# A two-layer decoder step on one core: the chunks of a loop body take their 264 columns in four orders

## What is computed

```python
def _layer(x, ...):
    xn = _rms_norm(x, g_pre_mix)
    proj = xn @ w_in                       # 2048 x IN_WIDTH
    ...                                    # retention, mLSTM, pooling on the parts of proj
    mixed = jnp.concatenate([ret_out, mlstm_out, pool_out], axis=-1).astype(x.dtype) @ w_out
    x = x + _rms_norm(mixed, g_post_mix)
    hn = _rms_norm(x, g_pre_ffn)
    ff = (jax.nn.silu(hn @ w_ffn_gate) * (hn @ w_ffn_up)) @ w_ffn_down
    x = x + _rms_norm(ff, g_post_ffn)
```

## Time and profile before

| | |
|---|---|
| two timed runs | 2467.01 and 2466.32 us, median 2466.66 us |
| the profiled execution, first to last instruction (its span) | 2466.6 us |
| TensorE, share of the span with a matmul in flight | 99% |
| TensorE, share of the span with a weight load in flight | 97% |
| VectorE, ScalarE, GpSimd, share of the span busy | 57%, 44%, 10% |
| mean granted TensorE clock over the span | 0.995 of full |
| bytes moved by DMA | 443.87 MB, mean 180 GB/s |

### The profile page before, as it was taken

The page is one execution under the profiler, slowest core; times in us unless marked ns, Lnnn a source line. Parts: engine busy times, 40 slices in busy tenths (PEclk is TensorE's granted clock), DMA queues, the critical chain, the costliest instruction groups (busy, mean ns, idle before and its releaser), DMA issues.

```text
span 2466.6 us, 49136 instructions
## 1 busy us (share of the span) xinstructions
PE 2435.6 (99%) x20166; PEld 2387.1 (97%) x20166; DVE 1417.3 (57%) x1721; ACT 1088.0 (44%) x1419; POOL 246.2 (10%) x202
## 2 busy tenths in 40 slices
PE   9999999999999999999999999999999999999997
PEld 8999999899999999999999999998999999999997
DVE  5787564755544455554567866646555445555444
ACT  5444654543333343444444456545344333343443
POOL 1001334000000000002100014340000000000021
PEclk9999999999999999999999999999999999999999
DMA  8455545355545655545645555454555455555453
GB/s 301 164 172 197 196 164 187 137 180 177 187 159 185 202 174 184 183 159 184 222 151 169 173 200 197 167 175 139 185 182 177 167 183 195 187 175 182 163 185 130
DMA packets 71902, 443.87 MB, mean 180 GB/s; under 512 B 8656, under 2 KB 8880, under 8 KB 33136
## 3 DMA queue, kind: packets, MB, share of 16 engines
q1 hardware_dynamic: 64656, 415.40, 49.6%
q0 software_dynamic: 6992, 26.82, 3.5%
q10 hardware_dynamic: 144, 0.08, 0.0%
HBM read 427.10 MB, written 15.16 MB: 179 GB/s over the span
## 4 chain that ended last, share of the span: by engine, by line
PE 95%; DVE 3%; ACT 1%; issue 0%; DMA 0%; DVEq 0%; ACTq 0%
PE bank L572 86%; PE bank L550 1%; PE bank L551 1%; PE bank L552 1%; PE bank L651 1%; DVE work L1326 1%; PE bank L539 0%; DVE x L1333 0%; DVE wlo L1306 0%; PE bank L603 0%; PE bank L604 0%; PE bank L622 0%; PE bank L514 0%; DVE rstd L1319 0%; PE bank L816 0%
## 5 line engine op out<-in xcount | busy, mean ns | idle before, releaser
L1306 DVE TENSOR_TENSOR wlo<-raw,whi 128x2048 fp32r<-128x2048 f32 (+1 forms) x402 | 836.8, 2082 | 512.7 <-ACT whi L941 512.5
L941 ACT ACTIVATE whi<-raw 128x2048 fp32r<-128x2048 f32 (+1 forms) x406 | 709.4, 1747 | 883.8 <-PE bank L572 833.2
L572 PE MATMUL bank<-ahi,wlo 128*128 128x264 f32 x4096 | 537.9, 284 | 0.0
L572 PE MATMUL bank<-ahi,whi 128*128 128x264 f32 x4032 | 533.3, 285 | 0.0
L572 PE MATMUL bank<-alo,whi 128*128 128x264 f32 x4032 | 528.3, 284 | 0.0
L572 PEld LDWEIGHTS bank<-ahi,wlo 128*128 128x128 f32 x4096 | 512.2, 188 | 0.0
L572 PEld LDWEIGHTS bank<-ahi,whi 128*128 128x128 f32 x4032 | 505.0, 188 | 7.1 <-issue 3.1
L572 PEld LDWEIGHTS bank<-alo,whi 128*128 128x128 f32 x4032 | 503.9, 188 | 0.0
L572 PE MATMUL bank<-hhi,wlo 128*128 128x264 f32 x1392 | 190.1, 284 | 0.0
L572 PE MATMUL bank<-hlo,whi 128*128 128x264 f32 x1392 | 188.7, 283 | 0.0
L572 PE MATMUL bank<-hhi,whi 128*128 128x264 f32 x1392 | 188.6, 283 | 0.0
(11 more groups left out here) (311 smaller groups left out, 1817.2 us busy)
## 6 DMA issues: line engine op xcount, KB each, us to landing
raw<-w_gu SPq DMA_DIRECT2D x176, 1024.0 KB, 4.8
raw<-w_in SPq DMA_DIRECT2D x89, 1024.0 KB, 5.0
raw<-w_dn SPq DMA_DIRECT2D x128, 704.0 KB, 4.0
raw<-w_out SPq DMA_DIRECT2D x32, 1024.0 KB, 4.9
work<-s_ret POOLq DMA_DIRECT2D x12, 512.0 KB, 3.7
ret_s<-work POOLq DMA_DIRECT2D x12, 512.0 KB, 3.0
proj<-s_c POOLq DMA_DIRECT2D x8, 576.0 KB, 5.5
c_s<-proj POOLq DMA_DIRECT2D x8, 576.0 KB, 4.1
```

The costliest lines, as they stand in the source:

```text
L572: mm = pe.matmul(out, weights[:, w], operand(tile)[of], start=start and part == 0 and k == 0, stop=stop and not late and part == 2 and k = ...
L941: act.activation(high[:, 0:words], raw[:, slot, 0:words], ACT.Copy).then_inc(*hi_made.up)
L1306: dve.tensor_tensor(wlo[:, slot, w], raw[:, slot, w], high[:, w].bitcast(F32), ALU.subtract)\
```

## The change

`chunk` gets a parameter `view`. A new helper `columns(view, ap)` rearranges the 264 columns of an access pattern: it cuts them into a parts of b blocks of c columns and goes through block 0 of each part, then block 1 of each part, and so on. View 0 leaves the pattern as it is; view 1 has 3 parts of 11 blocks of 8 columns, view 2 has 2 parts of 33 blocks of 4, view 3 has 2 parts of 66 blocks of 2. The helper is applied to the result's pattern in PSUM and to the streamed operand's in SBUF alike. `whole` passes view = j; all other callers keep view 0.

```diff
+                def columns(view, ap):
+                    if view:
+                        return ap.rearrange("p (a b c) -> p b a c", a=(1, 3, 2, 2)[view], c=(264, 8, 4, 2)[view])
+                    return ap
+
+                def chunk(n, slot, hi_slot, out, operand, ks, start, stop, last_ready=None, norm=None, middle=None, view=0):
+
+                    out = columns(view, out)
...
-                            mm = pe.matmul(out, weights[:, w], operand(tile)[of], start=start and part == 0 and k == 0,
+                            mm = pe.matmul(out, weights[:, w], columns(view, operand(tile)[of]), start=start and part == 0 and k == 0,
                                            stop=stop and not late and part == 2 and k == len(ks) - 1)
...
-                def whole_tile(c, o, slot, j, operand, hi_slot=0, norm=None, middle=None):
+                def whole_tile(c, o, slot, j, operand, hi_slot=0, norm=None, middle=None, view=0):
...
                     chunk(c, slot, hi_slot, bank[j][:, 0:TOK], operand, range(KT), True, True, norm=norm,
-                          middle=middle)
+                          middle=middle, view=view)
...
                             whole_tile(l * N_CHUNKS + c0 + i * RAW + j, l * N_TILES + o0 + i * RAW + j, (at_rest + j) % RAW, j, operand,
-                                       hi_slot=j % HI)
+                                       hi_slot=j % HI, view=j)
```

More of the change, by code:

```diff
@@ L555, in high_of @@
                     return whi_spare if hi_slot is None else whi[:, hi_slot]
-                def chunk(n, slot, hi_slot, out, operand, ks, start, stop, last_ready=None, norm=None, middle=None):
+                def columns(view, ap):
[4 more added lines that the diff above has]
+                    out = columns(view, out)
                     high, low = high_of(hi_slot), wlo[:, slot]
```

## The result

The changed kernel takes 2604.02 us (2602.32 to 2605.71, 2 runs) against 2466.66: 137 us more, ratio 1.0553 with a 95% interval of 1.0536 to 1.0570. The forecast was 2467 within 2425 to 2700, with 0.34 on slower. So the time is inside the range and outside the likeliest case, and it went the way to which 0.34 had been given.

The account below looks back on a forecast made before the run. The prediction took TensorE's matmul spacing in line 572 (120.8 ns, 86% of the span) as the bound. It summed 2466.6 us + 0 for all three reordered views to 2467 us, range 2425 to 2700.

Parts of the forecast that it names:

- 0.34 on slower: Whole kernel: chance 0.34 of being slower by over 2%, against 0.59 for within 2% and 0.07 for faster.
- the likeliest case: Loop chunks of `whole`: all four orders keep their spacing, time unchanged at 2467 us; chance 0.56.
- What bounds the kernel: Line 572, the matmul in `chunk`: its start-to-start spacing, 120.8 ns, is nearly the whole kernel; any change reaches the span undiminished.
- the 26 cycles of excess: Line 572 at 2.4 GHz: 10.8 ns of each 120.8 ns matmul are not columns, and come from the memory side.
- The half-clock rows: 264-column matmuls at 1.2 GHz start 220 ns apart, exactly 264 / 1.2, so the excess isn't a fixed instruction cost.
- rival E: Changed loop chunks: interleaving removes the excess, -9.5 ns on 6624 matmuls, -63 us, 2404 us; chance 0.09.
- The price of a run break: 6624 reordered loop matmuls: taken as 0 ns for all three orders, between bounds of -63 and +657 us.
- The second leg: VectorE and ScalarE rows: runs of 2 or more are free or nearly free at about one column a ns.
- The writes: TensorE's results in PSUM: 0 ns for the reordered patterns, though no row showed such a result in pieces.
- Rival B: Chunk 3 of each loop body: pairs fall to half rate, 2208 x 99.2 ns = 219 us, 2686 us; chance 0.15.
- Rival D: Loop chunks: excess grows with fetches; view 1 unchanged, view 2 twice, view 3 four times; +95 us, 2562; chance 0.12.
- Rival C: Views 1 to 3: any break, in reading or writing, halves the rate; +657 us, 3124 us; chance 0.08.

Follow-up runs that it names:

- The run with chunks at 236, 161, 197 and 154 ns: Changed kernel with loop chunks in pairs from 66 parts, sixes from 2, pairs from 3 and fours from 3, read and written: 3053.17 us.

## Why the prediction was right or wrong

*What bounds the kernel* was right: the spacing of line 572 accounts for 136.5 of the 137.4 us, so it arrived in the span whole, and the count of instructions stayed.

*That the 26 cycles of excess belong to the memory side* was right for 8.3 of the 10.8 ns, 20 of the 26 cycles; the run with repeated pieces shows it. The half-clock rows alone did not: the other 2.5 ns also vanish at 1.2 GHz, and they are there at 2.4 GHz with a single piece, so a spacing of exactly 264 / 1.2 is no proof of a slow supplier. For the same reason the floor for rival E was 112.5 and not 111.3 ns.

*The price of a run break, taken as 0 ns for all three orders*, is the step that failed: it was 3.2, 8.5 and 49.1 ns a matmul for views 1, 2 and 3, all on the reading side. It had two legs. The first was structural: the memory hands over a pair of neighbours at a time, so aligned pairs waste nothing. The runs show a unit of 16 bytes, four columns, at 1.8 ns per entry; a pair throws away half of what is fetched unless the other half is asked for almost at once. The second leg was the earlier trace rows, other engines reading runs of 2 at no extra cost. These read about one column a ns. By the measured 1.8 ns per entry, were it theirs too (which no run tried), two columns of theirs last about 2 ns, longer than a fetch, so it would be hidden even if each pair cost one. A row at 1 column a ns can say nothing of a stream that wants 2.4. I wrote that these rows were "suggestive, not conclusive" and then took their answer.

*The writes*: the same 0 ns was right for them (ratio 1.0001 with only the writes reordered).

*Rival B* had the right place, chunk 3, and the right mechanism (a pair costs a fetch of four columns), and a price twice too high: 219 us at 99.2 ns, where 49.1 ns were measured, 108 us. It assumed the full half rate; with two parts a piece is partly spared. The full price exists: from 66 parts it is 115 ns. *Rival D* came nearest in the total, 2562, by luck: it left view 1 unchanged (measured +3.2 ns), gave view 2 +10.8 (measured +8.5) and view 3 +32.4 (measured +49.1). Its reason does not hold for the first two, whose fetches are 66 as before; what differs there is only where consecutive fetches lie. *Rival C* is excluded by the write-only run and by runs of 8 at 124.0 ns. *Rival E*, relief by interleaving, was wrong for the orders of this change; another order, fours from 22 parts, gains 1.6 ns, 1.3% of the time, a sixth of the 9.5 ns it was priced at, for a reason that no run shows.

The range held because B and D were let into it, and not because the sum was near. The 0.34 on slower was too little: with 10% excess already on the memory side, the bound on a worse pattern was far wider than that on a better one, and my sum chose the middle by rows that did not bear on it.

## What to carry to other kernels

A streamed operand in rounded fp32 at full TensorE clock was bound here by 16-byte fetches of 1.8 ns. Walk it so that every piece is entered once and read whole; the order of the pieces then cost at most 9 ns of 121 here, except in steps of 6 or 22 pieces, which cost 34 to 40. A result in PSUM written in aligned pairs from two parts cost nothing. Before taking a price from another engine's rows, compare the rates: a cost that hides under 1 column a ns is bare at 2.4. And a spacing that equals columns over clock at the lower clock, but not at the higher one, is a hint at a supplier beside the engine, not a proof: here 8.3 of the 10.8 ns were the supplier's, and only reading the same piece again told them from the rest.

## What the runs showed of the hardware that was not expected

- The spacing of matmuls over 264 columns ran from 112.5 ns (pieces repeated) over 120.8 (consecutive) to 320.6 ns (pairs from 11 parts), with the same instructions and the same amount of arithmetic.
- The Trainium skill ("Advanced Engine Details and Errata", section "SBUF Cachelines") says that SBUF has 16-byte lines and that at least two hits on a line are needed to absorb the access latency. The 16 bytes agree with the 88 and 132 entries of the table. Two hits are not enough here: pairs that leave the line for 5 pieces or more, two fp32 hits each time, take 233 ns and more against 120.8.
- In the run with pairs from 6, 11, 33 and 22 parts the granted clock fell to 1.2 GHz in body after body though TensorE was in flight without a pause. In every body of the gate/up blocks the fall lies inside the chunk of 11 parts, whose matmuls start 321 ns apart, and the rise inside the chunk behind it. The run with chunks at 236, 161, 197 and 154 ns had no such falls. The falls cost nothing: the four spacings give 1,222 us (2208 x 553.3 ns), and the run took 1,222 us more than the kernel before. The windows of two stretches of pairs from 11 parts, at half and at full clock, and the timeline around the first:

```profile
1178.00:1188.00 10.00, 10.00 (x33) 10.00 (x33) 0.00 (x0) 0.00 (x0) 0.00 (x0) 0.50 0.00 0
...
1222.70:1226.70 4.00, 4.00 (x14) 2.81 (x13) 2.26 (x2) 2.23 (x2) 0.00 (x0) 1.00 0.64 215
...
1178.03 5.33 PE L578 MATMUL bank<-alo,whi 128*128 128x264 f32 x16
1183.16 5.33 PE L578 MATMUL bank<-ahi,wlo 128*128 128x264 f32 x16
...
1222.70 5.32 PE L578 MATMUL bank<-ahi,whi 128*128 128x264 f32 x16
1227.83 5.33 PE L578 MATMUL bank<-alo,whi 128*128 128x264 f32 x16
```

  16 matmuls take 5.13 us in the first stretch and in the second, which had the full clock for its first 4.0 us: 320.6 ns each. The clock does not set this pace, since 264 cycles of 1.2 GHz are only 220 ns.
